# Attention's values as the stationary operand in a two-layer hybrid decoder: outputs born transposed, probabilities normalised first, gates stored transposed

## The chip, the cores and the metric

One core of a Trainium2 chip runs the whole computation. The metric is the device time of one execution in microseconds (us); lower is better. A profile of one execution gives the spans of the instructions on TensorE (PE; its weight loads, PEld, are listed apart), VectorE (DVE), ScalarE (ACT), GpSimd (POOL) and SyncE (SP, which here only issues transfers and waits).

## The reference, cut to what matters

There are 16 meta tokens and 2048 tokens, each a row of 1024. A first layer (gated DeltaNet) gives the residual stream h. From it come one shared K and V (4 heads of 64), and for the second layer queries (16 heads of 64) and gates z (1024 wide). Each block of 128 queries sees the 16 meta tokens and a window of 128 back from each query, so the keys of the block before and its own.

```python
def sink_attention(q, k, v, mask, sinks):
    logits = einsum("bnqhgd,bnkhd->bnhgqk", q, k) * (SWA_HEAD_DIM ** -0.5)
    logits = where(mask, logits, NEG_BIG)
    m = maximum(max(logits, axis=-1, keepdims=True), s)      # s: one sink logit per head
    p = exp(logits - m)
    den = sum(p, axis=-1, keepdims=True) + exp(s - m)
    return einsum("bnhgqk,bnkhd->bnqhgd", p / den, v)
...
    o = o * silu(z)
    return o @ w_out            # added to h, then a final RMSNorm
```

All of it is float32. The kernel makes the large products of split operands: x = high + low, both in the type float32r, and high*high + high*low + low*high, which is three products for each slice of 128 of the contraction.

## The kernel before, in words

The kernel has four stages. The first two (up to some 1620 us) are the first layer. The change touches the third (`output_and_shared_kv`) and the fourth (`attention`). Each stage has one written-out program per engine; the engines run their own in order and wait for each other by semaphores, so the order of work on TensorE is the order of the calls in its `step`.

**Third stage, second loop** (from some 1854 to 2131 us): for each of the 16 token tiles T, TensorE makes K and V (24 products of 128x128 by 128x512), the gates' bank 0 (`gates(T, 0)`, 24), turns the keys (`turn_keys`, two transposes), and the gates' bank 1 (24). The gate is z times sigmoid(z): VectorE bounds z, ScalarE makes exp, log, exp (`gate_sigmoid`), VectorE multiplies into the tile `gate` (`gate_part`, L1747), and SyncE stores it to DRAM, 128 tokens by 1024 (L1565). The stage ends with the queries of tile 1 (`first_q`).

**Fourth stage**: `step(t, ...)` runs for t = -1 to 16, with the middle twelve steps in a loop. In a step TensorE makes the logits of tile t (`band_logits`, L2346: 64 rows of the contraction, one head, two heads on the two halves of the array's rows; `meta_logits`), the query projection of tile t+1 (L2315 into `first_q`, 48 products, of which 12 were made in the step before), and the output projection of tile t-1 (L2315 into `p_pso`, 48 products). VectorE and ScalarE merge and mask the logits, take the maximum (`maxima`), and ScalarE makes 16 exponentials with their sums (`exponentials`, L2080). The probabilities stand with queries on the partitions. They are transposed by TensorE (`turn_meta` for the 16 meta keys of all heads, `turn(t, g)` for group g of four heads; L2386, L2396), and VectorE writes them to `pT` twice, masked for the keys of the block before and for the block's own (`transposed`, L2210).

`values(t, s, g)` then makes probabilities times V: a transposed block of probabilities (128x128) is stationary and 64 columns of V move (L2417), eight products for each group, and one product of the 128 meta probabilities with a block-diagonal V of 128x512 for each bank of two groups (L2410). The profile shows each float32 product as two records. The output has queries on the partitions. VectorE multiplies it by the gates (`gate(t, b)`, L2218), GpSimd by one over the denominators (L2280), TensorE transposes it in eight pieces (`output_transposes`, L2357), ScalarE and VectorE split it into high and low (`output_high` L2090, `output_low` L2223), and the output projection takes these. VectorE adds the residual (L2231), ScalarE and GpSimd do the final norm.

The four calls of `values` are laid between pieces of the two projections. PSUM is full: `ps_q` (two banks) holds queries, then the attention's output; `ps_o` (two banks) holds in turn band logits, the transposed output, the projected output and the transposed queries.

## Time and profile before

| | |
|---|---|
| Median of 3 runs | 2870.61 us (2870.2 to 2880.4) |
| The profiled execution | 2870.26 us, span of its instructions 2868.5 us |
| Mean granted TensorE clock | 0.954 of full speed |
| Third stage, second loop | some 277 us, 16.6 us for a tile |
| Fourth stage | some 737 us, 43.5 us for a tile of the steady part |

A row of the timeline gives the start, the time from the first start to the last end of a run of like instructions, the engine, the line of the kernel, what is written and read, the shapes, and how many; in brackets the idle time of the engine before it and what ended it. For TensorE the ends are modelled (a product is written off some 0.2 us after its last column went in), so start to start is the better measure of what a run of products cost.

### The profile page before, as it was taken

Reading aid. Unit: us, or ns where it says so; the run is one execution under the profiler, and the core shown is the slowest. Engines: PE = TensorE matmul, PEld = TensorE weight load, DVE = VectorE, ACT = ScalarE, POOL = GpSimd, SP = SyncE. Lnnn points to the kernel's source line nnn. Section 1 sums busy time; section 2 is a strip of 40 time slices with the busy share of each in tenths; the row PEclk is TensorE's granted clock in tenths of the full one; section 3 lists DMA queues with packets and bytes.
Section 4 is the critical chain, followed back from the end, with each engine's and each line's share of the span. In section 5 each row is a group of like instructions: output and inputs, shape, how many; then the busy total and the mean of one; then the engine's idle time right before and its main releaser. Section 6 shows DMA issues by size and latency. Waiting matters only on the chain. (4 is left out here: it accounts for less than half of the span.)

```text
span 2868.5 us, 50727 instructions
## 1 busy us (share of the span) xinstructions
PE 2555.3 (89%) x17497; PEld 2265.2 (79%) x17497; DVE 1577.2 (55%) x3792; ACT 1115.9 (39%) x3278; POOL 478.3 (17%) x409
## 2 busy tenths in 40 slices
PE   5568878799999999999999599999978999999996
PEld 4467777789998999999998378788866887887875
DVE  4356666677777777777777223333324444444443
ACT  4244544444444444444444244333322323223232
POOL 0143343310000000000000022100002232233221
PEclk8789999999999999999999599999998999999998
DMA  6664344444445344444442267644553212112111
GB/s 199 194 235 146 123 164 146 142 154 129 140 142 194 117 156 130 130 133 156 127 130 72 89 220 256 221 152 161 213 220 120 67 66 74 59 64 82 59 49 46
DMA packets 273813, 392.78 MB, mean 137 GB/s; under 512 B 79282, under 2 KB 187906, under 8 KB 273442
## 3 DMA queue, kind: packets, MB, share of 16 engines
q1 hardware_dynamic: 240066, 370.05, 38.3%
q10 hardware_dynamic: 33632, 21.26, 2.5%
q8 instruction: 65, 1.06, 0.2%
q14 instruction: 50, 0.41, 0.0%
HBM read 267.92 MB, written 123.31 MB: 136 GB/s over the span
## 5 line engine op out<-in xcount | busy, mean ns | idle before, releaser
L1214 PE MATMUL p_psp<-xg,p_whi 128*128 128x264 f32 x4096 | 842.8, 296 | 21.7 <-POOL p_wlo L1163 19.3
L1214 PEld LDWEIGHTS p_psp<-xg,p_whi 128*128 128x128 f32 x4096 | 662.7, 193 | 24.9 <-issue 22.5
L1214 PE MATMUL p_psp<-xg,p_wlo 128*128 128x264 f32 x2048 | 611.8, 299 | 0.0
L1214 PEld LDWEIGHTS p_psp<-xg,p_wlo 128*128 128x128 f32 x2048 | 396.5, 194 | 0.0
L968 DVE SCALAR_TENSOR_TENSOR p_acc<-p_proj,p_taps,p_acc 128x528 f32<-128x528 f32 x288 | 251.3, 872 | 5.4
L1789 PE MATMUL first_q<-first_w,p_o 128*128 128x512 f32 (+1 forms) x864 | 207.0, 399 | 19.0 <-DVE first_w L1753 19.0
L2315 PE MATMUL first_q<-first_w,p_hT 128*128 128x512 f32 x720 | 199.9, 414 | 14.1 <-DVE p_q L2198 13.6
L1789 PEld LDWEIGHTS first_q<-first_w,p_o 128*128 128x128 f32 (+1 forms) x864 | 157.0, 184 | 62.6 <-issue 17.7
L849 ACT ACTIVATE p_sig<-p_sig 128x528 f32<-128x528 f32 x128 | 82.5, 644 | 296.1 <-DVE p_sig L970 295.8
L2315 PE MATMUL p_pso<-p_wo,p_oT 128*128 128x512 f32 x768 | 189.4, 400 | 5.1 <-DVE p_oT L2223 5.1
L1789 PE MATMUL p_psz<-p_wk,p_o 128*128 128x512 f32 x768 | 181.1, 392 | 0.0
L1010 DVE TENSOR_TENSOR p_prod<-p_Xb,p_blk 32x4 f32<-32x4 f32 (+13 forms) x448 | 169.8, 379 | 6.8
L2315 PEld LDWEIGHTS p_pso<-p_wo,p_oT 128*128 128x128 f32 x768 | 142.3, 190 | 37.2 <-DVE p_oT L2223 8.8
L1789 PEld LDWEIGHTS p_psz<-p_wk,p_o 128*128 128x128 f32 x768 | 142.9, 188 | 29.4
L2315 PEld LDWEIGHTS first_q<-first_w,p_hT 128*128 128x128 f32 x720 | 128.9, 192 | 43.6 <-issue 14.7
L1163 POOL TENSOR_TENSOR p_wlo<-p_wraw,p_whi 128x512 fp32r<-128x512 f32 x72 | 102.5, 1433 | 217.5 <-ACT p_whi L830 217.0
L2080 ACT ACTIVATE p_logits<-p_logits,p_top 128x144 f32<-128x144 f32 x256 | 102.6, 402 | 82.0 <-DVE p_top L2184 82.0
L2417 PEld LDWEIGHTS first_q<-p_v,p_pT 128*128 128x128 f32 x992 | 119.2, 192 | 16.6 <-issue 11.7
L1174 POOL TENSOR_TENSOR p_kg<-p_kT,p_er 128x512 f32<-128x512 f32 (+1 forms) x40 | 44.9, 1129 | 521.8 <-ACT p_er L866 521.7
L841 ACT ACTIVATE p_proj<-p_psp 128x264 f32<-128x264 f32 x256 | 99.6, 389 | 73.1 <-PE p_psp L1214 71.0
L2096 ACT ACTIVATE p_out<-p_h 128x1024 f32<-128x1024 f32 x16 | 17.0, 1060 | 279.0 <-DVE p_h L2231 279.0
L1179 POOL TENSOR_TENSOR p_qd<-p_qT,p_er 128x512 f32<-128x512 f32 (+1 forms) x40 | 51.2, 1288 | 439.0 <-DVE p_qT L990 439.0
(263 smaller groups left out, 4674.0 us busy)
## 6 DMA issues: line engine op xcount, KB each, us to landing
p_whi<-w_dram SPq DMA_DIRECT2D x92, 512.0 KB, 4.0
p_wlo<-w_dram SPq DMA_DIRECT2D x92, 512.0 KB, 4.9
p_wraw<-w_a_in SPq DMA_DIRECT2D x36, 512.0 KB, 6.6
w_dram<-p_whi SPq DMA_DIRECT2D x34, 512.0 KB, 4.1
w_dram<-p_wlo SPq DMA_DIRECT2D x34, 512.0 KB, 5.1
p_o<-hT_dram SPq DMA_DIRECT2D x34, 512.0 KB, 4.6
hT_dram<-p_hT SPq DMA_DIRECT2D x32, 512.0 KB, 3.4
p_hT<-hT_dram SPq DMA_DIRECT2D x30, 512.0 KB, 4.0
```

The costliest lines, as they stand in the source:

```text
L841: nc.scalar.activation(proj[:, f % 2, 3 + half_ * HALF:3 + (half_ + 1) * HALF], ps_p[half_][:, 0:HALF], ACT.Copy).then_inc(proj_read, 1)
L849: ins = nc.scalar.activation(v, v, ACT.Exp, scale=-1.0)
L968: nc.vector.scalar_tensor_tensor(a, p[:, part:part + GW], w, a, ALU.mult, ALU.add).then_inc(tap_done, 1)
L1010: link(nc.vector.tensor_tensor(t3, x3[:, 0:i, 0:i].rearrange("p j c -> p c j"), b3[:, 0:i, i].unsqueeze(1).to_broadcast([rows, i, i]), ALU ...
L1163: nc.gpsimd.tensor_tensor(w_lo[:, f, cols], w_raw[:, f % 2, cols], w_hi[:, f, cols].bitcast(f32), ALU.subtract).then_inc(lo_ready, 1)
L1174: nc.gpsimd.tensor_tensor(kg[p.par][:, at, :], cols(kT), e_r[:, at, :], ALU.mult).then_inc(keys_grown, 1)
L1179: nc.gpsimd.tensor_tensor(qd[p.par][:, at, :], cols(qT), e_r[:, at, :], ALU.mult).then_inc(queries_grown, 1)
L1214: ins = nc.tensor.matmul(ps_p[half_][:, 0:HALF], (w_hi, w_lo)[i][:, f, kc * P:(kc + 1) * P], xg[:, g % 2, j, kc, half_ * HALF:(half_ + 1) ...
L1789: last = nc.tensor.matmul(out, stationary[i][:, kc, 0:rows], moving(j, kc), start=kc == 0 and n == 0, stop=kc == KC - 1 and n == 2)
L2080: last_ = nc.scalar.activation(logits[:, s_, :], logits[:, s_, :], ACT.Exp, bias=top[:, s_:s_ + 1], accum_out=den[:, s_:s_ + 1])
L2315: ins = nc.tensor.matmul(banks[b][:], stationary[i][:, kc, :], weights[j][:, kc, b * FB:(b + 1) * FB], start=kc == 0 and n == 0, stop=kc = ...
L2417: last_ = nc.tensor.matmul(ps_q[b][:, cols], pT[:, g % 2, x, n * P:(n + 1) * P], v[:, slot, kvh * HD:(kvh + 1) * HD], start=False, stop=g ...
```

## The change

- `values`: V (128 keys by 64) is stationary, and the transposed probabilities move, 256 columns (two heads that share a KV head) at a time. The two KV heads of a bank write the two halves of the PSUM partitions. The meta part becomes eight products for each bank, 64 columns of the meta V stationary and 128 columns moving. The output now has features on the partitions and queries along the free axis: it is transposed already.
- `output_transposes` goes, and with it GpSimd's multiplication by one over the denominators. Instead VectorE normalises the probabilities (`normalise`: two multiplications of 128x8x144) before they are transposed.
- The gates have to have the same orientation. In the third stage TensorE transposes each gate tile (`turn_gates`, eight transposes), ScalarE copies it to `gT` (`gates_out`, two copies), and SyncE stores that, after the keys and not before them.
- The split into high and low reads the gated output in SBUF and not PSUM; ScalarE does its half ahead of the exponentials.
- In TensorE's order 24 products of the output projection stand ahead of `turn_meta` (none before), 6 between `turn` and the first `values`, 6 after it, 12 after the second.

The semaphore and buffer declarations are left out here.

```diff
+        gT = h1[:, 0, :].rearrange("p (c k) -> p c k", k=P)
...
-                if T >= 2:
-                    sp.wait_ge(gate_ready, 2 * (T - 1))
-                    sp.dma_start(gate_d[T - 2], gate[:]).then_inc(gate_out, 16)
                 if T < T_ALL:
                     sp.wait_ge(kT_ready, T + 1)
                     sp.dma_start(kT_d[T][:, :, 0:rows], kT[:, :, 0:rows]).then_inc(kT_out, 16)
+                if T >= 2:
+                    sp.wait_ge(gT_ready, 2 * (T - 1))
+                    sp.dma_start(gate_d[T - 2], gT).then_inc(gate_out, 16)
...
+            def gates_out(T):
+
+                act.wait_ge(gT_ps, T)
+                if T == 1:
+                    act.wait_ge(h1_out[0], 16 * (NT // 2))
+                else:
+                    act.wait_ge(gate_out, 16 * (T - 1))
+                for b in range(2):
+                    nc.scalar.activation(gT[:, 4 * b:4 * b + 4, :], ps_t[b][:].rearrange("p (c k) -> p c k", k=P),
+                                         ACT.Copy).then_inc(gT_ready, 1)
...
+                if T >= 2:
+                    gates_out(T - 1)
...
-                    dve.wait_ge(gate_out, 16 * (T - 1))
+                    dve.wait_ge(gT_ps, T - 1)
                 nc.vector.tensor_tensor(gate[:, b, :], ps_z[b][:], sig, ALU.mult).then_inc(gate_ready, 1)
...
+            def turn_gates(T):
+                pe.wait_ge(gate_ready, 2 * T)
+                if T > 1:
+                    pe.wait_ge(gT_ready, 2 * (T - 1))
+                for kc in range(KC):
+                    last = nc.tensor.transpose(ps_t[kc // 4][:, kc % 4 * P:(kc % 4 + 1) * P],
+                                               gate[:, kc // 4, kc % 4 * P:(kc % 4 + 1) * P], ident[:])
+                last.then_inc(gT_ps, 1)
...
                 gates(T, 0)
                 turn_keys(T)
+                if T > 1:
+                    turn_gates(T - 1)
                 gates(T, 1)
...
                 product(first_q[b][:], hT_in_sb[(T_ALL + 1) % 2], lambda j, kc: wq[j][:, kc, b * FB:(b + 1) * FB], P)
+                if b == 0:
+                    turn_gates(T_ALL - 1)
...
             def load_gate(t):
                 if not is_first(t):
-                    sp.wait_ge(oT_ps, t)
-                sp.dma_start(o[:], gate_d[t]).then_inc(gate_in, 16)
+                    sp.wait_ge(oT_lo, 2 * t)
+                sp.dma_start(oz[:], gate_d[t]).then_inc(gate_in, 16)
...
-                    if s_ == 0 and not is_first(t):
-                        act.wait_ge(gated, 2 * t)
...
             def output_high(t):
-                act.wait_ge(oT_ps, t + 1)
                 if not is_first(t):
                     act.wait_ge(h_ps, 2 * t)
                 for b in range(2):
-                    nc.scalar.activation(oT[0][:, 4 * b:4 * b + 4, :], grid(ps_o[b][:]), ACT.Copy).then_inc(oT_hi, 1)
+                    act.wait_ge(weighed, 2 * t + (b + 1))
+                    nc.scalar.activation(oT[0][:, 4 * b:4 * b + 4, :], oz[:, 4 * b:4 * b + 4, :],
+                                         ACT.Copy).then_inc(oT_hi, 1)
...
                     logits_in(t)
+                if last:
+                    output_high(t - 1)
                 if now:
                     exponentials(t)
-                if last:
-                    output_high(t - 1)
...
-            def denominators(t):
+            def normalise(t):
+
                 dve.wait_ge(probs_ready, t + 1)
+                dve.wait_ge(sink_ready, t + 1)
+                link(nc.vector.tensor_tensor(den[:], den[:], gap[:], ALU.add))
+                link(nc.vector.reciprocal(den[:], den[:]))
+                for b in range(2):
+                    sl = slice(8 * b, 8 * b + 8)
+                    nc.vector.tensor_tensor(logits[:, sl, :], logits[:, sl, :],
+                                            den[:, sl].unsqueeze(2).to_broadcast([P, 8, LW]), ALU.mult).then_inc(normalised, 1)
+                dve.wait_ge(normalised, 2 * (t + 1))
                 nc.vector.tensor_copy(pm[:].rearrange("p (h k) -> p h k", k=META), logits[:, :, P:LW]
                                       ).then_inc(pm_ready, 1)
-                dve.wait_ge(sink_ready, t + 1)
-                link(nc.vector.tensor_tensor(den[:], den[:], gap[:], ALU.add))
-                nc.vector.reciprocal(den[:], den[:]).then_inc(den_ready, 1)
...
-                nc.vector.tensor_tensor(o[:, b, :], ps_q[b][:], o[:, b, :], ALU.mult).then_inc(weighed, 1)
+                part = oz[:, 4 * b:4 * b + 4, :]
+                nc.vector.tensor_tensor(part, grid(ps_q[b][:]), part, ALU.mult).then_inc(weighed, 1)
 
             def output_low(t):
                 for b in range(2):
                     dve.wait_ge(oT_hi, 2 * t + (b + 1))
-                    nc.vector.tensor_tensor(oT[1][:, 4 * b:4 * b + 4, :], grid(ps_o[b][:]),
+                    nc.vector.tensor_tensor(oT[1][:, 4 * b:4 * b + 4, :], oz[:, 4 * b:4 * b + 4, :],
                                             oT[0][:, 4 * b:4 * b + 4, :].bitcast(f32), ALU.subtract).then_inc(oT_lo, 1)
...
                     query_bias(t + 1, 0)
-                if now:
-                    denominators(t)
                 if last:
                     output_low(t - 1)
                 if nxt:
                     query_bias(t + 1, 1)
+                if now:
+                    normalise(t)
                 if now:
                     transposed(t, (0, 1))
...
-                if now:
-
-                    pool.wait_ge(den_ready, t + 1)
-                    for b in range(2):
-                        pool.wait_ge(weighed, 2 * t + (b + 1))
-                        o3 = o[:, b, :].rearrange("p (h d) -> p h d", d=HD)
-                        nc.gpsimd.tensor_tensor(o3, o3, den[:, 8 * b:8 * b + 8].unsqueeze(2).to_broadcast([P, 8, HD]),
-                                                ALU.mult).then_inc(gated, 1)
...
-            def output_transposes(t):
-                pe.wait_ge(gated, 2 * (t + 1))
-                if not (isinstance(t, int) and t == NT - 1):
-                    pe.wait_ge(band_ready, 8 * (t + 2))
-                pe.wait_ge(qT_ready, 2 * (t + 2) if not (isinstance(t, int) and t == NT - 1) else 2 * NT)
-                for kc in range(KC):
-                    last_ = nc.tensor.transpose(ps_o[kc // 4][:, kc % 4 * P:(kc % 4 + 1) * P],
-                                                o[:, kc // 4, kc % 4 * P:(kc % 4 + 1) * P], ident[:])
-                last_.then_inc(oT_ps, 1)
...
                     if b == 0 and kc == 0:
+                        if not (isinstance(t, int) and t == NT - 1):
+                            pe.wait_ge(band_ready, 8 * (t + 2))
+                        pe.wait_ge(qT_ready, 2 * (t + 2) if not (isinstance(t, int) and t == NT - 1) else 2 * NT)
                         pe.wait_ge(oT_lo, 2 * (t + 1))
...
-                    nc.tensor.matmul(ps_q[b][:], pmT[:, b, :], vm[:, b, :], start=True, stop=False)
+                    for r in range(4):
+                        for i in range(2):
+                            nc.tensor.matmul(ps_q[b][i * HD:(i + 1) * HD, r * P:(r + 1) * P],
+                                             vm[:, b, (2 * r + i) * HD:(2 * r + i + 1) * HD], pmT[:, b, :],
+                                             start=r == 0, stop=False)
                 pe.wait_ge(pT_ready, 4 * t + (g + 1))
-                for n in range(4):
-                    kvh = 2 * b + n % 2
-                    cols = slice((4 * (g % 2) + n) * HD, (4 * (g % 2) + n + 1) * HD)
-                    for x, slot in ((0, 1 - s), (1, s)):
-                        if x or not is_first(t):
-                            last_ = nc.tensor.matmul(ps_q[b][:, cols], pT[:, g % 2, x, n * P:(n + 1) * P],
-                                                     v[:, slot, kvh * HD:(kvh + 1) * HD], start=False,
-                                                     stop=g % 2 == 1 and n == 3 and x == 1)
+                cols = slice(2 * (g % 2) * P, (2 * (g % 2) + 2) * P)
+                for x, slot in ((0, 1 - s), (1, s)):
+                    if x or not is_first(t):
+                        for i in range(2):
+                            kvh = 2 * b + i
+                            moving = pT[:, g % 2, x, :].rearrange("p (r i k) -> p r i k", r=2, i=2)[:, :, i, :]
+                            last_ = nc.tensor.matmul(ps_q[b][i * HD:(i + 1) * HD, cols].rearrange("p (r k) -> p r k", r=2),
+                                                     v[:, slot, kvh * HD:(kvh + 1) * HD], moving, start=False,
+                                                     stop=g % 2 == 1 and x == 1)
                 last_.then_inc(pv_ps, 1)
...
                     query_projection(t + 1, half, half + early // 2)
-                if last:
-                    output_transposes(t - 1)
                 if nxt:
                     query_projection(t + 1, half + early // 2, 2 * half)
+                if last:
+                    output_projection(t - 1, 0, half)
                 if now:
                     turn_meta(t)
                     turn(t, 0)
                     turn(t, 1)
                 if last:
-                    output_projection(t - 1, 0, early // 2)
+                    output_projection(t - 1, half, half + early // 2)
                 if now:
                     values(t, s, 0)
                 if last:
-                    output_projection(t - 1, early // 2, half)
+                    output_projection(t - 1, half + early // 2, half + early)
                 if now:
                     turn(t, 2)
                     values(t, s, 1)
                 if last:
-                    output_projection(t - 1, half, 2 * half)
+                    output_projection(t - 1, half + early, 2 * half)
...
-    "gate": [NT, P, 2, FB],
+    "gate": [NT, P, KC, P],
```

## Rows read from the trace of the kernel before

**Rows 1.** The page: busy time and share of the span of each engine.

```profile
PE 2555.3 (89%) x17497; PEld 2265.2 (79%) x17497; DVE 1577.2 (55%) x3792; ACT 1115.9 (39%) x3278; POOL 478.3 (17%) x409
```

**Rows 2.** Windows: stretch, its length, busy us (instructions) of each engine, clock, DMA share, GB/s.

```profile
1854.00:2131.00 277.00, 276.69 (x1234) 227.73 (x1232) 97.38 (x163) 82.90 (x129) 0.00 (x0) 1.00 0.48 172
...
2192.00:2798.30 606.30, 587.25 (x3881) 487.06 (x3880) 275.18 (x574) 181.59 (x644) 172.30 (x153) 1.00 0.19 65
2798.30:2868.50 70.20, 46.07 (x279) 38.86 (x278) 21.81 (x44) 15.86 (x51) 9.20 (x7) 0.83 0.14 47
```

**Rows 3.** Timeline of TensorE over one tile of the fourth stage's steady part.

```profile
2453.05 1.16 PE L2346 MATMUL p_psr<-p_kT,p_qT 64*128 64x128 f32 x16
2454.14 0.97 PE L2315 MATMUL first_q<-first_w,p_hT 128*128 128x512 f32 x3
...
2457.84 0.96 PE L2315 MATMUL first_q<-first_w,p_hT 128*128 128x512 f32 x3
2458.72 1.16 PE L2346 MATMUL p_psr<-p_kT,p_qT 64*128 64x128 f32 x16
...
2461.80 2.34 PE L2315 MATMUL first_q<-first_w,p_hT 128*128 128x512 f32 x9
2464.81 1.09 PE L2357 MATMUL p_pso<-p_ident,p_o 128*128 128x128 f32 x8 [0.67 <-DVE p_logits L2169]
2465.66 4.37 PE L2315 MATMUL first_q<-first_w,p_hT 128*128 128x512 f32 x18
2470.53 0.44 PE L2386 MATMUL p_psm<-p_ident,p_pm 128*128 128x128 f32 x2 [0.50 <-DVE p_pm L2188]
...
2472.05 1.66 PE L2315 MATMUL p_pso<-p_wo,p_oT 128*128 128x512 f32 x6 [0.21 <-DVE p_oT L2223]
2473.55 1.02 PE L2410 MATMUL first_q<-p_vm,p_pmT 128*128 128x512 f32 x2
2474.40 1.89 PE L2417 MATMUL first_q<-p_v,p_pT 128*128 128x64 f32 x16
2476.11 4.36 PE L2315 MATMUL p_pso<-p_wo,p_oT 128*128 128x512 f32 x18
2480.30 0.60 PE L2396 MATMUL p_psr<-p_ident,p_logits 128*128 128x128 f32 x4
...
2496.58 1.16 PE L2346 MATMUL p_psr<-p_kT,p_qT 64*128 64x128 f32 x16
```

**Rows 4.** Timeline of TensorE in the second stage, one product with 64 stationary columns.

```profile
809.18 0.65 PE L1293 MATMUL p_psl<-p_Xt,p_half 128*64 128x64 f32 x8 [0.29 <-ACT p_Xt L894]
```

**Rows 5.** Timeline of VectorE in the same tile as rows 3.

```profile
2466.75 0.69 DVE L2198 TENSOR_TENSOR p_q<-first_q,p_bq 128x512 f32<-128x512 f32 x1
...
2470.12 0.35 DVE L2188 COPY p_pm<-p_logits 128x256 f32<-128x256 f32 x1 [2.68 <-ACT p_logits L2080]
...
2470.59 0.25 DVE L2192 RECIPROCAL p_den<-p_den 128x16 f32<-128x16 f32 x1
```

**Rows 6.** One line's instructions: duration in ns, minimum, median, maximum.

```profile
L1716 DVE TENSOR_TENSOR p_hT<-p_hn,p_hT x8: 1224/1226/1227, 1994.8 to 2111.8; 128x1024 fp32r<-128x1024 f32 x8
```

**Rows 7.** Timeline of TensorE in the third stage's second loop.

```profile
1997.78 0.38 PE L1833 MATMUL p_psk<-p_ident,p_work 128*128 128x128 f32 x2
1997.92 5.74 PE L1789 MATMUL p_psz<-p_wk,p_o 128*128 128x512 f32 x24
```

**Rows 8.** Timeline of VectorE in the same tile as rows 7.

```profile
2000.70 0.69 DVE L1747 TENSOR_TENSOR p_gate<-p_psz,p_work 128x512 f32<-128x512 f32 x1 [2.03 <-ACT p_work L1647]
```

**Rows 9.** Timeline of TensorE in tile 0, the last tile and behind it.

```profile
2180.37 0.45 PE L2386 MATMUL p_psm<-p_ident,p_pm 128*128 128x128 f32 x2 [0.25 <-DVE p_pm L2188]
...
2814.83 0.69 PE L2386 MATMUL p_psm<-p_ident,p_pm 128*128 128x128 f32 x2 [3.66 <-DVE p_pm L2188]
...
2834.59 3.68 PE L2417 MATMUL first_q<-p_v,p_pT 128*128 128x64 f32 x32
...
2845.40 12.66 PE L2315 MATMUL p_pso<-p_wo,p_oT 128*128 128x512 f32 x48 [2.01 <-DVE p_oT L2223]
```

More of the change, by code:

```diff
@@ L1438, in output_and_shared_kv @@
         v_out = sem("p3_v_out")
+        gT_ps = sem("p3_gT_ps")
+        gT_ready = sem("p3_gT_ready")
         gate_out = sem("p3_gate_out")
@@ L1884, in attention @@
         pmT = sb("p4_pmT", [P, 2, P])
-        o = sb("p4_o", [P, 2, FB])
+        oz = sb("p4_oz", [P, KC, P])
         oT = [sb(f"p4_oT{n}", [P, KC, P], f32r) for n in range(2)]
@@ L1929, in attention @@
         sink_ready = sem("p4_sink_ready")
-        den_ready = sem("p4_den_ready")
+        normalised = sem("p4_normalised")
         pT_ps = sem("p4_pT_ps")
@@ L1938, in attention @@
         scaled = sem("p4_scaled")
-        gated = sem("p4_gated")
-        oT_ps = sem("p4_oT_ps")
         oT_hi = sem("p4_oT_hi")
```

## The prediction

> **What bounds the kernel now.** I read the page's first part, then the windows by stage, then TensorE's timeline of one tile in attention, then VectorE's of the same tile, and last the stages at both ends of the change.
>
> TensorE is busy 89% of the span [rows 1]. The change touches two stages, and both are TensorE's: from 1854 to 2131 us it is busy 276.69 of 277 us, and in attention's steady part 587.25 of 606.30 us, at the full clock (PEclk 1.00) in both; only the last 70 us are looser, with a clock of 0.83 [rows 2]. VectorE is busy 275 and ScalarE 182 of those 606 us. So an instruction taken from TensorE's row there is worth its slot, and one given to it costs its slot; work of the others counts only where TensorE then waits. One tile of attention takes 43.53 us, from one first band product to the next (2453.05 to 2496.58) [rows 3]; the tiles 1 to 14 fill the 606 us.
>
> TensorE is full there but for three places [rows 3]. Nine query products start at 2461.80 and at 0.233 us each, with some 0.1 for the switch out of the band form, are done at about 2464.0; the eight output transposes go 2464.81 to 2465.66 and the next 18 products begin there: a slot of 1.6 us. These 18 take 4.19 (so do the 18 from 2476.11 to 2480.30), to 2469.85, but the next transposes start at 2470.53: 0.68 lost, on the copy of the meta probabilities. Those ten transposes, 0.107 each, end at 2471.60, and the output projection starts at 2472.05: 0.45 lost, on VectorE's split of the transposed output.
>
> **The price of a column-tiled product.** After the change values are 128x64 stationary and 256 columns of probabilities move; two such products (i = 0, 1) write different halves of the PSUM partitions. No row shows two halves side by side. The nearest rows: a record of 512 float32 columns takes 0.43 (two in 2473.55 to 2474.40), so 256 take 0.213 and 128 take 0.107 [rows 3]. The band products are halves too, of the rows: 16 records of 128 columns would take 1.71 one by one; they took 1.09 (2453.05 to 2454.14) [rows 3]. That is 0.86, in pairs, and 0.23 for the switch; the three products between two bands take 0.88 (2457.84 to 2458.72) where 0.70 is their due, another 0.18. So halves of the rows run together and a visit to the form costs 0.4. Halves of the columns: L1293 (128x64 stationary, 64 columns moving) has one half only, and its eight records took 0.65, at most 0.08 each [rows 4], where today's values with 128 stationary columns take 0.107 for the same 64 moving (16 in 2474.40 to 2476.11) [rows 3]: a 64-column weight load is the cheaper one and hides behind the product before it.
>
> I take "two halves run together, 0.4 a visit", as with the band. Values of one group: eight records of 0.213, 0.86 in pairs, 1.71 one by one; before 1.71 (2474.40 to 2476.11). The meta product of one bank: 16 records of 0.107, again 0.86 in pairs and 1.71 one by one; before 0.85.
>
> The Trainium skill ("TensorE: Matmul & The Clock Gate", Part 3) has three column tiles at 2.38 times one, which would support this; the sum does not use it. The same section says that a weight load overlaps running matmuls only where the row group differs, and all these products use all rows. By that rule each record would pay its load; what this would make is the second rival. The trace speaks against it: L1293's 64-column records follow one another at no more than 0.08 each [rows 4], load and product of the same rows together.
>
> **The change part by part, per steady tile.**
> - Output transposes gone: 1.6 us.
> - Waits of 0.68 and 0.45 gone: 24 output products (24 x 0.233 = 5.6) now stand ahead of turn_meta. 1.1 us, if what follows is in time.
> - Values: four groups, 6.9 before; now 4 x 0.86 + 4 x 0.4, less 0.2 as the last visit runs straight into the next band: 4.8. Meta: nothing either way. 2.1 us gained.
> - A new wait. The projection now needs VectorE's output_low, which stands behind query_bias. TensorE is ready at 2464.0 + 4.2 = 2468.2. VectorE's bias add runs 2466.75 to 2467.44 [rows 5], then two subtractions of 512 (1024 take 1.23 [rows 6], so 0.6 each) to 2468.65; with the signal 2468.8. Cost 0.6. Behind it on TensorE stands all of the rest; nothing else fills it. ScalarE's copies run in its idle time after the band.
> - normalise. Probabilities are ready at 2470.1 as now [rows 5]. Then sum and reciprocal to 2470.8 (2470.59 + 0.25), two multiplications of 1152 elements (at 1.2 per 1000: 1.36, the second 1.25 after the first) to 2473.4, and the meta copy, 0.35, to 2473.8. TensorE comes to turn_meta at 2468.8 + 5.6 = 2474.4. Hidden with 0.6 to spare; without the cover it would be 3.3 us a tile. VectorE grows by 2.6 us in 43.5 and has room.
> - Gating moves from GpSimd after VectorE to VectorE alone; the gate load now waits for output_low, at 2468.7, with 12 us until gate(t,0). Nothing.
> - Later pT masks: turn(t,3) is near 2485, its masks done near 2487, values(t,3) wanted near 2490. Nothing.
>
> Sum: 1.6 + 1.1 + 2.1 - 0.6 = 4.2 a tile, a period of 39.3; 14 tiles: -58.8 us.
>
> **The other stages.** In the stage before, eight transposes per tile go between turn_keys and gates(T, 1), where TensorE has not a gap (1997.78, 1997.92) [rows 7]. At 0.83 (0.85 for the eight of rows 3) times 16: +13.3. Not less, for nothing is removed there; more only if someone waits. VectorE's product for bank 0 is at 2000.70 [rows 8], the transposes would be done at 1998.9; ScalarE is busy 83 of 277 us, so two copies (17 us in all) fit; SP's gate store comes some 3 us after the key store instead of ahead of it, and the hT load behind it is wanted a tile later. Nothing.
>
> Tile 0 has no projection to cover normalise: TensorE's wait that ends at 2180.37 [rows 9] would end at 2183.7: +3.3; its values are half as many, a little less. Net +3.
>
> The last tile: TensorE waits there for probabilities until 2814.8 [rows 9], so 24 output products move into the hole, but turn_meta is 3 us later, at about 2819.5; I work out the values' end 3.7 earlier. Behind it, from the end of the values (2838.2) to 2845.40 [rows 9] lie a gating, GpSimd, eight slow transposes and the split, 7.2 us; now a gating 0.69, a copy 0.58, a subtraction 0.6 and signals, 2.2: 5 us. A shorter hole may spare slow products (0.8 of 1.4 possible). -9.5.
>
> Together: -58.8 + 13.3 + 3 - 9.5 = -52. The profiled execution took 2870.26 us (span 2868.5), the median is 2870.61, which is the same. 2818 us.
>
> **Rivals.**
> - *One by one* (slower). The halves of the columns don't run together. Values 4 x 1.71 + 1.4 = 8.2 instead of 4.8, meta 1.7 more: 5.1 a tile lost against the forecast, so -4.2 + 5.1 = +0.9, 14 tiles +13; tile 0 +4.5, last -5, transposes +13.3: 2896. For it: no row of two column halves; only the rows' halves are shown. Against: the array evidently takes parts. It decides from 3.7 us a tile lost on.
> - *Together, but the loads show*: each record pays about 0.06 for its 64-column load. Values +0.24 a group at least with pairs kept, 0.48 without; meta 0.5 to 1 a bank: 2 to 4 a tile, and 2846 to 2874. [rows 4] are against it. The Trainium skill's overlap rule above would give this.
> - *normalise shows in steady state*: VectorE 1 to 2 us later than I sum (GpSimd rotates at the same time), so that turn_meta waits 0.5 to 1.5 us a tile: 2825 to 2839.
> - Switches that cost 0.2 or 0.6 instead of 0.4: 11 us either way.
>
> **How the numbers follow.** Forecast 0.70 (own range 2805 to 2835), normalise shows 0.07, loads show 0.09, one by one 0.14. The range goes from 2803 to 2860: it takes in the first two and half of the third, and leaves out one by one and a little more. 0.5% (14 us) is about what a measurement can tell; faster than 2856: 0.70 + 0.07 + 0.03 = 0.80; within: 0.06; slower: 0.14.
>
> **What would show it.** In the new profile's steady tile: records of L2417's successor marked 128*64 with pairs starting within some ns, a values group of 1.2 to 1.3 us, and a period near 39.3. TensorE idle about 0.6 before the first output product, on VectorE's oT, and none before turn_meta. In the stage before, eight more transposes per tile and a period 0.83 longer. If the records of a group start 0.21 apart, singly, the first rival holds. It is wrong, too, if turn_meta waits on the meta copy, or if masks or gates come late after values got shorter.

## The result, and the profile after

The change makes the kernel faster by 0.8%: 2851.13 us median of 4 runs (2846.97 to 2854.87) against 2870.4 of the kernel before in the same rounds; ratio 0.992, 95% interval 0.9906 to 0.9935. The forecast was 2818 us. The sign and the mechanism on TensorE were right, the size was not: 19 us came, 52 were forecast. The profiled execution is the slowest of the four (2854.87 us, span 2853.1), so its span is only 15.4 us under the span before.

The page's first part, after; it answers to [rows 1]:

```profile
PE 2520.7 (88%) x17449; PEld 2201.3 (77%) x17449; DVE 1665.2 (58%) x3824; ACT 1134.3 (40%) x3310; POOL 487.8 (17%) x377
```

VectorE has 88 us more than before, TensorE 35 less. The windows, cut at the end of the third stage and at the first band products of tile 1 and of the last tile, in the columns of [rows 2]:

```profile
2148.90:2220.10 71.20, 40.76 (x191) 29.88 (x190) 20.53 (x34) 10.93 (x40) 17.95 (x16) 0.66 0.50 193
2220.10:2790.90 570.80, 537.72 (x3714) 412.17 (x3713) 356.07 (x603) 184.17 (x644) 183.87 (x126) 1.00 0.20 69
2790.90:2853.10 62.20, 40.24 (x258) 31.86 (x258) 25.96 (x46) 15.88 (x51) 6.10 (x3) 0.84 0.16 53
```

The tiles 1 to 14 take 570.8 us where they took 606.3 [rows 2], so 35.5 less, not 58.8. The last part takes 62.2 where it took 70.2: 8 less, 9.5 were forecast. VectorE is busy 356 us in the steady part and was 275; GpSimd 184, and was 172 though a multiplication has been taken from it. TensorE over one steady tile, after:

```profile
2260.85 1.16 PE L2371 MATMUL p_psr<-p_kT,p_qT 64*128 64x128 f32 x16
...
2269.60 6.42 PE L2340 MATMUL first_q<-first_w,p_hT 128*128 128x512 f32 x27
2277.03 5.73 PE L2340 MATMUL p_pso<-p_wo,p_oT 128*128 128x512 f32 x24 [1.01 <-DVE p_oT L2256]
2284.11 0.44 PE L2404 MATMUL p_psm<-p_ident,p_pm 128*128 128x128 f32 x2 [1.35 <-DVE p_pm L2223]
2284.38 1.04 PE L2414 MATMUL p_psr<-p_ident,p_logits 128*128 128x128 f32 x8
...
2286.75 1.09 PE L2430 MATMUL first_q<-p_pmT,p_vm 128*64 128x128 f32 x16
2287.67 1.03 PE L2440 MATMUL first_q<-p_pT,p_v 128*64 128x256 f32 x8
2288.64 1.65 PE L2340 MATMUL p_pso<-p_wo,p_oT 128*128 128x512 f32 x6
...
2301.82 0.38 PE L2371 MATMUL p_psr<-p_kT,p_qT 64*128 64x128 f32 x2
```

The tile is 40.97 us (2260.85 to 2301.82), 2.56 less than the 43.53 of [rows 3]. L2440 is values, L2430 the meta part, both marked 128*64. A group of values took 0.97 (2287.67 to 2288.64), before 1.71; the meta part 0.92. What was to be gained there was gained. Within the group the records start in pairs, 7 ns apart (2287.672 and 2287.679), and the pairs follow 0.216 us apart: the sign of two halves running together that the prediction had named. What is new are two waits in brackets: 1.01 for `oT` (L2256, the split) and 1.35 for `pm` (L2223, the meta copy behind normalise). The forecast had 0.6 and nothing. VectorE in that tile, after, against [rows 5]:

```profile
2275.15 1.82 DVE L2256 TENSOR_TENSOR p_oT<-p_oz,p_oT 128x512 fp32r<-128x512 f32 x2
...
2278.09 0.88 DVE L2216 TENSOR_TENSOR p_den<-p_den,p_gap 128x16 f32<-128x16 f32 x1 [0.52 <-ACT p_gap L2108]
...
2279.29 4.03 DVE L2220 TENSOR_TENSOR p_logits<-p_logits,p_den 128x1152 f32<-128x1152 f32 x2
2283.36 0.70 DVE L2223 COPY p_pm<-p_logits 128x256 f32<-128x256 f32 x1
```

And GpSimd, which rotates the next queries at the same time:

```profile
2275.32 1.11 POOL L2320 TENSOR_TENSOR p_swapped<-p_q,p_cs 128x256 f32<-128x256 f32 x1 [15.48 <-DVE p_q L2230]
...
2277.64 1.29 POOL L2324 TENSOR_TENSOR p_q<-p_q,p_cs 128x512 f32<-128x512 f32 x1
2279.01 1.28 POOL L2326 TENSOR_TENSOR p_q<-p_q,p_swapped 128x512 f32<-128x512 f32 x1
2280.44 1.67 POOL L2320 TENSOR_TENSOR p_swapped<-p_q,p_cs 128x256 f32<-128x256 f32 x1
2282.07 1.83 POOL L2321 TENSOR_TENSOR p_swapped<-p_q,p_cs 128x256 f32<-128x256 f32 x1
```

The two multiplications of normalise took 4.03 together, not 2.6; the sum of 16 numbers 0.88, where it began during GpSimd's L2324 and ended with it (2278.97 and 2278.93). GpSimd's half rotations, 0.73 before, took 1.1 to 1.8. The two engines end in turn: GpSimd at 2280.30, the first multiplication at 2281.51, GpSimd at 2282.11, the second multiplication at 2283.32, GpSimd at 2283.90, the meta copy at 2284.05. A multiplication ends 1.21 us after GpSimd's operation before it, and a half 0.6 after VectorE's, each a little less than it takes alone (1.35 and 0.73): the one works only when the other has all but ended, and the wait stands in the record as a longer duration and not as idle time. The meta copy has a single input, in SBUF, and is held up too: 0.70 here, 0.29 in the next run. Over all tiles, with minimum, median and maximum in ns:

```profile
L2220 DVE TENSOR_TENSOR p_logits<-p_logits,p_den x32: 1352/1895/2233, 2201.5 to 2809.0; 128x1152 f32<-128x1152 f32 x32
```

The minimum, 1352, is that of the last tile, where no queries are rotated.

In the third stage the transposes lie where they were put; the rows answer to [rows 7]:

```profile
2130.44 0.38 PE L1849 MATMUL p_psk<-p_ident,p_work 128*128 128x128 f32 x2
2130.66 1.04 PE L1858 MATMUL p_pst<-p_ident,p_gate 128*128 128x128 f32 x8
2131.45 5.71 PE L1805 MATMUL p_psz<-p_wk,p_o 128*128 128x512 f32 x24
```

Eight take 0.79. In tile 0 and behind the last tile:

```profile
2206.26 0.69 PE L2404 MATMUL p_psm<-p_ident,p_pm 128*128 128x128 f32 x2 [5.86 <-DVE p_pm L2223]
...
2830.73 12.54 PE L2340 MATMUL p_pso<-p_wo,p_oT 128*128 128x512 f32 x48 [4.19 <-DVE p_oT L2256]
```

Tile 0 waits 5.86 us for the meta copy (0.25 in [rows 9]) and takes 47.4 us where it took 36.1: 11.2 more, forecast 3.

### The profile page after: what moved, and what is told of

The parts are those of the page before. It is cut to its first block and busy times, and to the rows that moved or that the text cites. A ratio compares the mean times of both kernels' runs of the same rounds, so it can differ in the third digit from the quotient of the medians.

```text
span 2853.1 us, 50697 instructions
## 1 busy us (share of the span) xinstructions
PE 2520.7 (88%) x17449; PEld 2201.3 (77%) x17449; DVE 1665.2 (58%) x3824; ACT 1134.3 (40%) x3310; POOL 487.8 (17%) x377
## 5 line engine op out<-in xcount | busy, mean ns | idle before, releaser
L1805 PE MATMUL first_q<-first_w,p_o 128*128 128x512 f32 (+1 forms) x864 | 207.2, 399 | 20.8 <-DVE first_w L1769 20.8
L2340 PE MATMUL p_pso<-p_wo,p_oT 128*128 128x512 f32 x768 | 195.4, 404 | 25.8 <-DVE p_oT L2256 25.8
L1805 PEld LDWEIGHTS first_q<-first_w,p_o 128*128 128x128 f32 (+1 forms) x864 | 157.0, 184 | 64.2 <-issue 18.4
L1805 PE MATMUL p_psz<-p_wk,p_o 128*128 128x512 f32 x768 | 181.2, 392 | 0.0
L1805 PEld LDWEIGHTS p_psz<-p_wk,p_o 128*128 128x128 f32 x768 | 142.9, 188 | 29.1
L2320 POOL TENSOR_TENSOR p_swapped<-p_q,p_cs 128x256 f32<-128x256 f32 x32 | 41.7, 1304 | 593.7 <-DVE p_q L2230 591.5
L1012 DVE TENSOR_REDUCE p_Xb<-p_prod 32x2 f32<-32x4 f32 (+13 forms) x448 | 105.1, 235 | 15.4
```

The source lines that it names most:

```text
L1012: link(nc.vector.tensor_reduce(x3[:, i, 0:i], t3, mybir.AxisListType.X, ALU.add))
L1805: last = nc.tensor.matmul(out, stationary[i][:, kc, 0:rows], moving(j, kc), start=kc == 0 and n == 0, stop=kc == KC - 1 and n == 2)
L2340: ins = nc.tensor.matmul(banks[b][:], stationary[i][:, kc, :], weights[j][:, kc, b * FB:(b + 1) * FB], start=kc == 0 and n == 0, stop=kc = ...
```

## The experiments

**Rotation after normalise.** Is it GpSimd that holds VectorE up, or is the multiplication dear in itself?

```diff
 # GpSimd, step
+                if now:
+                    pool.wait_ge(normalised, 2 * (t + 1))
                 if nxt:
                     rotate(t + 1, 1 - s)
```

> The changed kernel, with one wait more: GpSimd begins the rotation of tile t+1's queries only when VectorE has normalised tile t. Theory A (VectorE's operations with two inputs in SBUF and GpSimd's rotation hold each other up): the two multiplications of normalise fall from 2.2 and 1.9 us to 1.36 each in every tile, the split's second subtraction from 1.2 to 0.7, GpSimd's halves from 1.1 to 1.8 us back to 0.73; TensorE's wait before turn_meta falls from 1.4 us to under 0.3, before the first output product from 1.0 to 0.5; the tile from 40.98 to about 39.2 us, 14 tiles 24 us, tile 0 one to three us: 2823 to 2828 us. Theory B (the multiplication by a broadcast operand itself takes 1.9 us): durations and the tile stay as they are, 2851, or longer since the rotation is later. The rotation would then end near 8.5 us after normalise, some 6 us before the queries' transposes, so it should cost nothing by either.

2821.36 us median (2820.11 to 2823.26, 4 runs), ratio to the kernel before 0.9814 (0.9798 to 0.9831): 30 us under the changed kernel, for a wait added. VectorE, the same place in a tile, then all 32 multiplications:

```profile
2310.69 0.18 DVE L2216 TENSOR_TENSOR p_den<-p_den,p_gap 128x16 f32<-128x16 f32 x1 [1.04 <-ACT p_gap L2108]
...
2311.19 2.63 DVE L2220 TENSOR_TENSOR p_logits<-p_logits,p_den 128x1152 f32<-128x1152 f32 x2
2313.85 0.29 DVE L2223 COPY p_pm<-p_logits 128x256 f32<-128x256 f32 x1
```

```profile
L2220 DVE TENSOR_TENSOR p_logits<-p_logits,p_den x32: 1349/1354/1360, 2200.4 to 2775.9; 128x1152 f32<-128x1152 f32 x32
```

The run adds a wait and takes nothing away. From the sum's start to the end of the meta copy it is 3.45 us, where it was 5.97 (2278.09 to 2284.06); every multiplication takes 1.35. TensorE:

```profile
2302.20 6.42 PE L2342 MATMUL first_q<-first_w,p_hT 128*128 128x512 f32 x27
2309.19 5.73 PE L2342 MATMUL p_pso<-p_wo,p_oT 128*128 128x512 f32 x24 [0.57 <-DVE p_oT L2256]
2314.76 0.38 PE L2406 MATMUL p_psm<-p_ident,p_pm 128*128 128x128 f32 x2
...
2332.41 1.16 PE L2373 MATMUL p_psr<-p_kT,p_qT 64*128 64x128 f32 x16
```

In tiles 1 to 14 no wait is left ahead of turn_meta, and 0.3 to 0.6 ahead of the first output product; tile 0 still waits 4.14 us for the meta copy. The steady part takes 541.99 us for 14 tiles, 38.7 each, which is 64.3 less than before the change, where 58.8 were forecast. Theory A stands: what VectorE and GpSimd hold up in each other is 2.1 us a tile. Windows of that run, tile 0 and tiles 1 to 14, in the columns of [rows 2]:

```profile
2173.46:2215.79 42.33, 31.35 (x170) 23.31 (x170) 14.66 (x28) 8.55 (x37) 8.02 (x8) 0.73 0.33 129
2215.79:2757.78 541.99, 534.63 (x3714) 413.35 (x3712) 313.39 (x603) 184.21 (x644) 143.76 (x126) 1.00 0.21 72
```

The Trainium skill ("SBUF — State Buffer", Who interferes with whom) says this: a VectorE instruction with two inputs in SBUF and a GpSimd instruction that reads SBUF exclude each other, and the second to start waits. The trace agrees (the ends in turn above), and shows the other side too: the masks, with one input in PSUM, keep their 0.68 beside GpSimd's L2326, and GpSimd its 1.29. The two in the timeline of this run:

```profile
2315.66 1.29 POOL L2326 TENSOR_TENSOR p_q<-p_q,p_cs 128x512 f32<-128x512 f32 x1
```

```profile
2315.70 0.69 DVE L2242 TENSOR_TENSOR p_pT<-p_psr,p_before_T 128x512 f32<-128x512 f32 x1 [1.56 <-PE p_psr L2416]
```

**Both KV heads on one half.** What is running side by side worth?

```diff
-  nc.tensor.matmul(ps_q[b][i * HD:(i + 1) * HD, ...], ...)
+  nc.tensor.matmul(ps_q[b][0:HD, ...], ...)
```

The flags that open and close a sum are set to match. The second half of the PSUM partitions is left out: both heads add into the first.

> The changed kernel with every product of values writing the same half of the columns (both KV heads into PSUM partitions 0 to 63), so the attention's output is wrong there; the number, the sizes and the order of the products are as in the changed kernel. It prices the products one by one. The run with the halves in turn showed that records far apart in the order still ran side by side where they use different halves; here there is only one half. Theory A (the gain comes from the two halves running side by side): a group of values goes from 0.97 to 1.8 us, a bank's meta part from 0.92 to 1.75, 4 x 0.85 + 2 x 0.83 = 5.1 us a tile, 14 tiles 71 us: about 2922 us. Theory B (a product with 64 stationary columns is cheap by itself): within 10 us of 2851.

(The run with the halves in turn, which this text refers to, is the next section.)

2927.15 us (one run). Values and meta part in TensorE's timeline of this run:

```profile
2296.59 1.94 PE L2440 MATMUL first_q<-p_pT,p_v 128*64 128x256 f32 x8
2298.46 3.02 PE L2340 MATMUL p_pso<-p_wo,p_oT 128*128 128x512 f32 x12
...
2302.78 1.96 PE L2430 MATMUL first_q<-p_pmT,p_vm 128*64 128x128 f32 x16
2304.58 1.89 PE L2440 MATMUL first_q<-p_pT,p_v 128*64 128x256 f32 x8
```

A group takes 1.87, a bank's meta part 1.80, the tile 46.2 us; the eight records of a group follow singly, most 0.216 us apart, which is about the due of 256 columns alone (0.213 in the prediction). The two halves side by side are worth 5.2 us a tile and some 76 in all; without that, the change would have been slower than the kernel before by 53 (2873.76 in those rounds). Theory A holds.

**One half after the other.** Must neighbours in the order use different halves?

```diff
-                    for r in range(4):
-                        for i in range(2):
+                    for i in range(2):
+                        for r in range(4):
...
-                for x, slot in ((0, 1 - s), (1, s)):
-                    if x or not is_first(t):
-                        for i in range(2):
+                for i in range(2):
+                    for x, slot in ((0, 1 - s), (1, s)):
+                        if x or not is_first(t):
```

> The changed kernel with the loops over i turned outward in values: all products of one half of the columns, then all of the other, and not in alternation. Theory A (two products run together only where neighbours in the order use different halves): a group of values goes from 0.97 to about 1.7 us, the meta part of a bank from 0.92 to about 1.7, so 4 x 0.75 + 2 x 0.8 = 4.6 us a tile, 14 tiles 64 us: about 2915 us. Theory B (each half has a queue of its own, or the gain does not come from running together): no change, 2851.

2867.26 us (one run), 41.94 us a tile: 1 us more, not 4.6. Theory A as I put it falls; the first form of theory B, a queue for each half, is nearest, though not to the end (its second form, that nothing runs together, falls with the run before). TensorE's timeline of this run, one tile:

```profile
2330.40 1.25 PE L2430 MATMUL first_q<-p_pmT,p_vm 128*64 128x128 f32 x13
2331.39 0.43 PE L2440 MATMUL first_q<-p_pT,p_v 128*64 128x256 f32 x1
2331.49 0.38 PE L2430 MATMUL first_q<-p_pmT,p_vm 128*64 128x128 f32 x2
...
2332.78 1.65 PE L2340 MATMUL p_pso<-p_wo,p_oT 128*128 128x512 f32 x6
...
2334.80 1.09 PE L2440 MATMUL first_q<-p_pT,p_v 128*64 128x256 f32 x8
2335.82 3.02 PE L2340 MATMUL p_pso<-p_wo,p_oT 128*128 128x512 f32 x12
```

A group without meta still takes 1.02, with four records of one half ahead of the four of the other. With the meta part (eight records of a half, then eight), 2.38 are needed, where it was 1.89. And a record of L2440, which stands behind all of L2430 in the order, starts at 2331.39 while three records of L2430 have yet to start (2331.49, 2331.60, 2331.71). So a product can start ahead of an earlier one that waits for the other half; how far ahead TensorE can look is not shown. The run also answers a rival to the run before, where both heads add into one place: that the place in PSUM, and not the half, keeps the products apart. Here the first records of the meta part all write one half, each product other columns, and they follow singly, 0.11 apart (2330.56, 2330.67, 2330.78, 2330.89). It is the half. There is one execution of this run; twelve of its fourteen steady tiles are 41.93 to 41.96 us long.

**The output projection late.** What is "sooner" worth?

```diff
-                if last:
-                    output_projection(t - 1, 0, half)
                 if now:
                     turn_meta(t)
...
```

> The changed kernel with the output projection where it was: no product ahead of turn_meta, 6 before the first values, 18 after, 24 after the second. What the sooner projection is worth: TensorE would wait from the end of the query products to the meta copy's end, 2276.0 to 2284.1 in the tile shown, 8.1 us, where it now waits 2.4 in two places; 5.6 us a tile more, 46.6 us, 14 tiles 79 us: about 2930 us, slower than before the change. If normalise did not set the start of turn_meta, nothing would change: 2851.

The first 24 output products go back behind turn_meta, to where 6, 18 and 24 stood before the change. 2954.7 us (one run), 47.8 us a tile: 6.9 a tile more, not 5.6. TensorE's timeline in a steady tile of this run, and a window around it in the columns of [rows 2]:

```profile
2480.07 0.69 PE L2404 MATMUL p_psm<-p_ident,p_pm 128*128 128x128 f32 x2 [8.02 <-DVE p_pm L2223]
2480.55 1.92 PE L2414 MATMUL p_psr<-p_ident,p_logits 128*128 128x128 f32 x8
```

```profile
2476.00:2483.00 7.00, 2.92 (x12) 2.83 (x13) 5.25 (x6) 0.38 (x1) 6.26 (x5) 0.53 0.41 164
```

TensorE waits 8.02 us for the meta copy, 5.7 more than the two waits of the changed kernel together. The rest is the clock: from 2476.4 to 2483.3, in the second half of that wait and behind it, half of full speed (1.2 GHz) is granted (0.53 over the window), and the eight transposes take 1.92 with their tail where they took 1.04. The 24 products ahead of turn_meta carry the change as much as the halves do (104 us in this run, 76 in the one on one half).

**Gates not turned.** What do the transposes in the third stage cost?

```diff
-                if T > 1:
-                    turn_gates(T - 1)
...
-                if b == 0:
-                    turn_gates(T_ALL - 1)
...
-                    nc.scalar.activation(gT[...], ps_t[b][:]...)
+                    nc.scalar.activation(gT[...], gate[:, b, :]...)
```

> The changed kernel without the 16 x 8 transposes of the gates: ScalarE copies the gate tile as it is, so the output is gated by the wrong gate elements; all else is as in the changed kernel. If the transposes cost their slots on TensorE (0.79 us for eight) and nothing else: 12.6 us less, 2838 us, and the third stage's tile back from 17.4 to 16.6 us. If ScalarE's copies or the later store had cost something besides: less than 12.6 comes back. The fourth stage keeps its 40.98 us.

2843.65 us median (2837.1 to 2844.9, 4 runs), ratio to before 0.9886 (0.9866 to 0.9905); against the changed kernel's 0.992 (0.9906 to 0.9935) the intervals just miss each other, and the medians differ by 7 to 10 us, so the runs alone don't tell 12.6 from less. The traces do. First and last start of the gates' products (L1805, `p_psz`), changed kernel, this one, and before the change:

```profile
L1805 PE MATMUL p_psz<-p_wk,p_o x768: 389/389/500, 1864.0 to 2136.8; 128*128 128x512 f32 x192
```

```profile
L1805 PE MATMUL p_psz<-p_wk,p_o x768: 387/389/500, 1868.1 to 2128.0; 128*128 128x512 f32 x192
```

```profile
L1789 PE MATMUL p_psz<-p_wk,p_o x768: 387/389/500, 1859.5 to 2119.4; 128*128 128x512 f32 x192
```

272.8, 259.9 and 259.9 us: 12.9 for the 15 turns between, 0.86 each, and ScalarE's copies and the later store, which this run keeps, cost nothing. In this run's fourth stage a tile takes 40.98, as expected.

**Rotation after normalise, and the split first.** What is late next?

```diff
 # VectorE, step, on top of the rotation after normalise
+                if last:
+                    output_low(t - 1)
                 if nxt:
                     query_bias(t + 1, 0)
-                if last:
-                    output_low(t - 1)
```

> The run with the rotation after normalise, and VectorE's output_low ahead of query_bias(t+1, 0). There TensorE still waited 0.57 us before the first output product, for the second subtraction, with the bias add (0.6) ahead of it. If that order is the whole of the wait: the wait goes, the tile falls from 38.92 to about 38.4 us, 14 tiles 7 us, and a little in the last tile: about 2813 us. If something else would be late next (the masks merged, the normalised probabilities before turn_meta, which would then be wanted 0.5 us sooner with about 0.1 us to spare): the wait moves there and the time stays at 2821.

2814.83 us median (2812.82 to 2818.43, 5 runs), ratio to the kernel before 0.9792 (0.9778 to 0.9805), the lowest median of all. Its interval overlaps that of the rotation after normalise alone (0.9798 to 0.9831), so it is the traces that tell the two apart: tiles 1 to 14 take 535.7 us where they took 542.0, and the tile is 38.47 us.

```profile
2303.94 5.72 PE L2342 MATMUL p_pso<-p_wo,p_oT 128*128 128x512 f32 x24
2309.62 0.44 PE L2406 MATMUL p_psm<-p_ident,p_pm 128*128 128x128 f32 x2
```

The wait for the split is gone from tiles 1 to 14, and none has come ahead of turn_meta (24 products begin at 2303.94 and the transposes at 2309.62, 5.68 for their due of 5.6).

## Why the prediction was right in sign and wrong in size

The forecast's parts against the traces, in us (profiled spans; the run with the rotation after normalise in the last column):

| part | forecast | changed kernel | rotation after normalise |
|---|---|---|---|
| up to tile 0's first band product | +13.3 | +16.9 | +17.6 |
| tile 0 | +3 | +11.2 | +6.2 |
| tiles 1 to 14 | -58.8 | -35.5 | -64.3 |
| last tile and end | -9.5 | -8.0 | -6.5 |
| sum | -52 | -15.4 | -47.0 |

- **Values side by side, 0.4 a visit**: right. A group was taken at 1.26 with its switches and measured 0.97 to 1.02 and some 0.1 to 0.2 on its neighbours. So the rival of cheaper switches (11 us faster) came true in part, which is why the last column has 64.3 and not 58.8; in the changed kernel this gain hides some 5 us of what the waits cost. For the products one by one the run on one half gives 1.87 for a group. My price for "one by one", 2896 us, was too low (2927), since I had priced its groups and not the waits that came besides.
- **Transposes gone, two waits gone**: the transposes are gone. The waits for the meta copy and for the split are not: both are back, longer (1.35 and 1.01), for the reasons in the next two points. With the rotation held back and the split first neither is left in tiles 1 to 14.
- **"normalise. ... Hidden with 0.6 to spare"**: this is the step that failed. The 1.36 us for a multiplication came from a multiplication with GpSimd idle [rows 6], and was applied to a place where GpSimd rotates, which I had named only in a rival at 0.07 and priced at up to 1.5 us a tile in one wait. From the sum's start to the meta copy's end it was 5.97 us; the forecast had 3.7 from the ready probabilities. So turn_meta waits 1.35 us. With the rotation held back the meta copy ended at 2314.14 and turn_meta began at 2314.76: 0.6 to spare, as forecast. The sum was right for the durations that it took, and these don't hold beside GpSimd.
- **"A new wait ... Cost 0.6"**: 1.0 measured, and 0.57 in the tile shown with the rotation held back: the same cause (the second subtraction held up by the rotation). From the start of the query products to that of the output products, and from there to turn_meta, it took 7.43 and 7.08 us, with the rotation held back 6.99 (2302.20 to 2309.19) and 5.57: 1.95 a tile, 27 us in 14 tiles. That is shown by the run, which gives 29 us back in tiles 1 to 14. They lack only 23 against the forecast, since the values came out cheaper; 8 of the other 13 us that the profiled span lacks are in tile 0.
- **Tile 0, +3**: +11.2. The wait there is 5.86 us and not some 3.5 (0.25 before and 3.3 more); with the rotation held back it is 4.14 and tile 0 5 us shorter. Part of the rest is the clock, which I had not put a price on: full speed came back at 2172.8 before the change and at 2195.5 in the changed kernel, and behind the wait half of it (1.2 GHz) is granted from 2205.7 to 2212.5. The products from the meta logits to the wait take 2.0 us more for it, and all that stands behind the wait 2.2. And 1.0 to 1.4 us more pass between the first band product and the meta logits, which wait for the meta values from DRAM; why is not shown.
- **Third stage, +13.3**: its cause is measured at 12.9 in the loop and 0.8 behind it. The other 3 us up to tile 0 came ahead of the first turned gate. The gates' products begin at 1864.0 and not 1859.5: before them TensorE waited 4.19 us for VectorE where it had waited 3.67, half of full speed (1.2 GHz) was granted from 1854.1 to 1861.0 where the clock had stayed full, and 24 products of K and V took 8.1 us where they took 5.6. The products before that wait had begun 1.5 us later already (1844.8 and 1843.3). Of these 4.5 us, 1.4 are gained back between the loop's end and tile 0. All seven profiles with the change have such a fall of the clock, the one profile before has none; whether the change brings it is not shown. The first band product of tile 0 lies between 2170.4 and 2175.2 in the six of them that turn the gates.
- **Last tile, -9.5**: -8.0. Behind the values TensorE waits 4.19 us where I had 2.2. The first half of VectorE's last split took 2.4 us while GpSimd made the final norm of the tile before: by the ends (GpSimd's at 2829.43, the half's at 2829.98) the same exclusion once more, though no run tests it here. The two in the changed kernel's timeline:

```profile
2827.56 3.02 DVE L2256 TENSOR_TENSOR p_oT<-p_oz,p_oT 128x512 fp32r<-128x512 f32 x2 [0.21 <-ACT p_oT L2115]
```

```profile
2827.09 2.35 POOL L2306 TENSOR_TENSOR p_out<-p_out,p_final 128x1024 f32<-128x1024 f32 x1 [34.78 <-ACT p_out L2125]
```

What stays open: how far ahead TensorE looks for a product of the other half, why the meta values come later in tile 0, and why the clock falls at the head of the third stage's loop. Of the 6.2 us that tile 0 still takes more than before with the rotation held back, 3.9 are the wait for the meta copy, 1.0 the wait for the meta values, and 1.3 slower products.

## What to carry to other kernels

- A duration of a VectorE instruction with two inputs in SBUF holds only for what GpSimd does beside it; the meta copy, float32 from SBUF to SBUF, shows the same (0.29 and 0.70). Before such an instruction is put on the path that TensorE waits for, lay GpSimd's timeline under its place, and move the GpSimd work that has slack: here one wait more made the kernel 30 us faster.
- Products with 64 stationary columns are worth the change only if two of them write different halves of the PSUM partitions; by themselves they cost more here than the form that they replace (1.87 for 1.71 a group, 1.80 for 0.85 a meta part).
- Where an operation is put between two TensorE steps, the work that covers it is part of the change: without the 24 products ahead of turn_meta the same kernel is some 3% slower than before.

## What the runs showed of the hardware that was not expected

- VectorE and GpSimd stretched each other: multiplications of 1352 ns to 1895 (median) and 2233 (longest), GpSimd's 0.73 us halves to 1.8, a sum of 16 numbers 0.17 to 0.88, a subtraction of 0.68 to 2.4, a copy of 0.29 to 0.70 and, in tile 0, 1.23. The second to start ended a little less than its own duration after the first (1.21 and 0.6 us), so it waited for nearly the whole of it.
- Eight records of values on two halves took 0.97 us where on one half they took 1.87, and a product may start ahead of an earlier one of the other half. The Trainium skill ("TensorE: Matmul & The Clock Gate", Part 3) has products in strict order, and in its list of what overlaps it has weight loads overlapping running products only where the row group differs. The first does not fit 2331.39 above. The second does not fit the records on one half: each loads its own 64 columns, all use all rows, and they still follow at 0.216 us, about the due of 256 columns. The measurement decides.
